# Row norm in the attention, one block for the finish, and two early loads, in a hybrid decoder layer on one core

## What is computed

```python
h = rmsnorm(x, g_mix_pre); proj = h @ w_in            # q, k, v and the RWKV inputs
o_att = attend(q, k4, v, lam)                         # differential attention, 4 heads of 128
o_att = rmsnorm(o_att, g_subln) * (1 - lam_init)      # per head and token
# RWKV: y from the delta-rule scan, 8 heads of 64
y = (y - mean) * rsqrt(var + GN_EPS)                  # per head and token
y = y * ln_x_w + ln_x_b
y = (y + bonus) * g
mix = concat([o_att, y]) @ w_o
x = x + rmsnorm(mix, g_mix_post)
x = x + rmsnorm(conv_ffn(rmsnorm(x, g_ffn_pre)), g_ffn_post)
x = x + rmsnorm((pe @ w_ple) * sigmoid(x @ w_ple_gate), g_ple)
```

## Time and profile before

| | us |
|---|---|
| median of 3 runs | 2096.89 (2096.22 to 2100.23) |
| profiled execution, device time | 2095.08 |
| its span | 2093.3 |
| mean granted clock of TensorE | 0.938 |
| TensorE busy | 1875.1 (90%) |
| VectorE busy | 1056.6 (50%) |
| ScalarE busy | 788.2 (38%) |
| GpSimd busy | 281.3 (13%) |

### The profile page before, as it was taken

One profiled execution on the slowest core, in us unless ns is written; L12 is line 12 of the kernel. 1 busy time (PEld: TensorE's weight loads), 2 busy tenths in 40 slices (PEclk: granted clock), 3 DMA queues, 4 the chain that ended last, 5 costly groups with the idle time before them and its releaser, 6 DMA issues.

```text
span 2093.3 us, 46480 instructions
## 1 busy us (share of the span) xinstructions
PE 1875.1 (90%) x19772; PEld 1781.1 (85%) x19772; DVE 1056.6 (50%) x1828; ACT 788.2 (38%) x1358; POOL 281.3 (13%) x288
## 2 busy tenths in 40 slices
PE   6999999599997488875499899999999999999996
PEld 5888888599996366664499899999999999999996
DVE  4355544235444466632326586654336766523655
ACT  4243323023320355531234555443335555422442
POOL 0011112069950000003000000000000000000000
PEclk9999999899999688886599999999999999999998
DMA  4234333620010877531124243323433422333343
GB/s 151 98 127 147 122 106 127 243 57 4 4 25 12 226 216 222 171 133 46 51 90 154 77 148 122 120 90 110 134 124 122 165 92 91 99 112 111 112 134 104
DMA packets 100620, 240.73 MB, mean 115 GB/s; under 512 B 14210, under 2 KB 18434, under 8 KB 100130
## 3 DMA queue, kind: packets, MB, share of 16 engines
q1 hardware_dynamic: 99554, 234.55, 35.0%
q10 hardware_dynamic: 864, 3.24, 0.4%
HBM read 189.54 MB, written 48.21 MB: 114 GB/s over the span
## 4 chain that ended last, share of the span: by engine, by line
PE 46%; DVE 2%; ACT 1%; issue 1%; DMA 0%; POOL 0%; SPq 0%; ACTq 0%; DVEq 0%
PE tl_acc L1970 44%; PE tl_ple L1970 1%; PE tl_wide L1945 0%; PE tl_wide L1936 0%; ACT tl_wh L2119 0%; DVE tl_tmp L2244 0%; DVE tl_gated L2307 0%; DVE tl_gated L2310 0%; DMA tl_raw<-dram_w_o 0%; ACT tl_sq_e L1982 0%; DVE tl_Y L2226 0%; DVE tl_Y L2217 0%; ACT tl_Hh L2088 0%; DVE tl_acc_e L2150 0%; DVE tl_wl L2290 0%
## 5 line engine op out<-in xcount | busy, mean ns | idle before, releaser
L1970 PE MATMUL tl_acc<-tl_Hh,tl_wh 128*128 128x264 f32 x1536 | 440.1, 287 | 7.3 <-DVE tl_Hl L2248 7.3
L1970 PE MATMUL tl_acc<-tl_Hh,tl_wl 128*128 128x264 f32 x1536 | 438.3, 285 | 0.0
L1970 PE MATMUL tl_acc<-tl_Hl,tl_wh 128*128 128x264 f32 x1536 | 438.2, 285 | 0.0
L2290 DVE TENSOR_TENSOR tl_wl<-tl_raw,tl_wh 128x1024 fp32r<-128x1024 f32 (+2 forms) x184 | 208.4, 1132 | 427.2 <-ACT tl_wh L2119 427.1
L2119 ACT ACTIVATE tl_wh<-tl_raw 128x1024 fp32r<-128x1024 f32 (+2 forms) x184 | 181.0, 984 | 503.0 <-PE tl_acc L1970 454.0
L1970 PEld LDWEIGHTS tl_acc<-tl_Hh,tl_wh 128*128 128x128 f32 x1536 | 290.3, 189 | 8.5 <-DVE tl_Hl L2248 8.3
L1970 PEld LDWEIGHTS tl_acc<-tl_Hh,tl_wl 128*128 128x128 f32 x1536 | 291.3, 190 | 0.0
L1970 PEld LDWEIGHTS tl_acc<-tl_Hl,tl_wh 128*128 128x128 f32 x1536 | 290.7, 189 | 0.0
L1970 PE MATMUL tl_acc<-tl_Gl,tl_wh 128*128 128x264 f32 x704 | 200.3, 285 | 0.0
L1970 PE MATMUL tl_acc<-tl_Gh,tl_wl 128*128 128x264 f32 x704 | 200.1, 284 | 0.0
L1970 PE MATMUL tl_acc<-tl_Gh,tl_wh 128*128 128x264 f32 x704 | 200.0, 284 | 0.0
(11 more groups left out here) (355 smaller groups left out, 4431.8 us busy)
## 6 DMA issues: line engine op xcount, KB each, us to landing
tl_raw<-dram_w_up SPq DMA_DIRECT2D x88, 512.0 KB, 3.6
...
```

Of the source, the lines that this page charges most:

```text
L1970: last = nc.tensor.matmul(out[:, n, 0:HP], w[:, u % 2, k, :], z, start=(begin and q == 0), stop=(end and q == 2))
L2290: tt(wl[:, u % 2, 0:kt], raw[:, u % 3, 0:kt], wh[:, u % 2, 0:kt].bitcast(F32), ALU.subtract).then_inc(S["residued"], 1)
```

## The change

- In the attention the first head's q and k are loaded and split inside the scan: SyncE issues the four loads, ScalarE makes the four high parts, GpSimd the four low parts. `dup`, `qs`, `kh` and `kl` are allocated outside of both stages.
- A block's weights are no longer scaled by 1/sum0: `wgt = p0 + p1 * (coefficient * sum0)`, one operation in place of two. `values` swaps its operands, so that a block's output has tokens on the partitions, and `leave` applies 1/sum0, once with a square that also sums along the row, and once as a copy.
- The attention's norm is taken from these sums: `root_rows`, `norm_rows`, `turn_rows` (eight transposes) and `keep_rows` (a copy with the gain), in the next head's steps 2, 3, 4 and 5. For the last head they stand at the end, together with the samples'. A head is stored whole.
- `rwkv_finish`, the small block, `rms_rows` and both `scale_split` become one block, `finish_rows`. The variance is made by a full-width matmul; root and reciprocal (`scale`, on VectorE) run over all 1056 columns; the bias is added to the bonus by GpSimd; the splits of O and Y into `Mh` and `Ml` stand in it.
- In the same block the first three units of `w_o` are loaded and two of them split; `tail` begins with unit 2.

```diff
-def attend(kit, a, proj, oT, ident, identb, causal, lam):
+def attend(kit, a, proj, oT, ident, identb, causal, lam, eps, g_subln, dup, qs, kh, kl):
...
-        dup = kit.sb(ctx, "ap_dup", [P, 2, 2, SEQ])
-        qs = kit.sb(ctx, "ap_qs", [P, 2, 2, SEQ], F32R)
-        kh = kit.sb(ctx, "ap_kh", [P, 2, 2, SEQ], F32R)
-        kl = kit.sb(ctx, "ap_kl", [P, 2, 2, SEQ], F32R)
...
             def load_qk(h):
-                if h:
-                    sp.wait_ge(S["low"], h * 4)
+                if h >= 2:
+                    sp.wait_ge(S["low"], (h - 1) * 4)
...
+            def store(h):
+                sp.wait_ge(S["o_kept"], h + 1)
+                sp.dma_start(oT[h][:, 0:SEQ], out[:]).then_inc(S["o_stored"], 16)
...
-            load_qk(0)
...
+                if s % NQ == 6 and 0 < h:
+                    store(h - 1)
+            store(HEADS - 1)
...
+                elif i == 3 and h:
+                    pe.wait_ge(S["o_kept"], h)
...
-                    last = nc.tensor.matmul(pv[:, 0:P], vt[:, h % 2, n, :], wT[:, s % 2, n, :],
+                    last = nc.tensor.matmul(pv[:, 0:P], wT[:, s % 2, n, :], vt[:, h % 2, n, :],
...
+            def turn_rows(h):
+                pe.wait_ge(S["normed"], h + 1)
+                pe.wait_ge(S["kept"], min(NQ * (h + 1) + 3, U))
+                for n in range(NQ):
+                    last = nc.tensor.transpose(tp[:, n, :], orow[:, h % 2, n, :], ident)
+                last.then_inc(S["o_turned"], 1)
...
+                if s % NQ == 4 and s >= NQ:
+                    turn_rows(s // NQ - 1)
...
-                nc.vector.tensor_scalar(small[:, b, 8:9], small[:, b, 7:8], neg_lam, None,
-                                        ALU.mult).then_inc(S["coefd"], 1)
+                nc.vector.tensor_scalar(small[:, s % 4, 8:9], small[:, s % 4, 7:8], neg_lam, small[:, s % 4, 4:5],
+                                        ALU.mult, ALU.mult).then_inc(S["coefd"], 1)
...
-                nc.vector.tensor_scalar(wgt[:, b, 0:keys], pexp[:, b, 0, 0:keys], small[:, b, 6:7], None,
-                                        ALU.mult).then_inc(S["w_first"], 1)
...
-                nc.vector.scalar_tensor_tensor(wgt[:, b, 0:keys], pexp[:, b, 1, 0:keys], small[:, b, 8:9],
-                                               wgt[:, b, 0:keys], ALU.mult, ALU.add).then_inc(S["weighted"], 1)
+                nc.vector.scalar_tensor_tensor(wgt[:, b, 0:keys], pexp[:, b, 1, 0:keys], small[:, s % 4, 8:9],
+                                               pexp[:, b, 0, 0:keys], ALU.mult, ALU.add).then_inc(S["weighted"], 1)
...
+            def norm_rows(h):
+                dve.wait_ge(S["rooted"], h + 1)
+                groups = slice(h % 2, h % 2 + (1 if h < HEADS - 1 else 2))
+                nc.vector.reciprocal(rms[:, groups], rms[:, groups]).then_inc(S["o_inverted"], 1)
+                dve.wait_ge(S["o_inverted"], h + 1)
+                nc.vector.tensor_tensor(orow[:, h % 2], orow[:, h % 2], rms[:, h % 2].unsqueeze(2).broadcast_to([P, NQ, P]),
+                                        ALU.mult).then_inc(S["normed"], 1)
...
+                if s % NQ == 3 and s >= NQ:
+                    norm_rows(s // NQ - 1)
...
+            norm_rows(HEADS - 1)
+            nc.vector.tensor_tensor(rows_out[:], rows_out[:], rms[:, 2].unsqueeze(2).broadcast_to([P, NB, P]),
+                                    ALU.mult).then_inc(Z["normed"], 1)
...
             def leave(s):
-                g, at = s // 4, (s % 4) * P
+                h, i = s // NQ, s % NQ
                 act.wait_ge(S["summed"], s + 1)
-                if s % 4 == 0 and g >= 2:
-                    act.wait_ge(half_out[g % 2], (g // 2) * 16)
-                nc.scalar.activation(out[:, g % 2, at:at + P], pv[:, 0:P], ACT.Copy).then_inc(S["evacuated"], 1)
+                if i == 0 and h >= 2:
+                    act.wait_ge(S["o_turned"], h - 1)
+                act.wait_ge(S["inverted"], s + 1)
+                if s:
+                    act.wait_ge(S["squared"], s)
+                nc.scalar.activation(sq[:], pv[:, 0:P], ACT.Square, scale=small[:, s % 4, 6:7],
+                                     accum_out=rms[:, h % 2, i:i + 1]).then_inc(S["squared"], 1)
+                nc.scalar.activation(orow[:, h % 2, i], pv[:, 0:P], ACT.Copy, scale=small[:, s % 4, 6:7])\
+                    .then_inc(S["evacuated"], 1)
+
+            def root_rows(h):
+                act.wait_ge(S["squared"], NQ * (h + 1))
+                groups = slice(h % 2, h % 2 + (1 if h < HEADS - 1 else 2))
+                if h == HEADS - 1:
+                    act.wait_ge(Z["squared"], NB)
+                nc.scalar.activation(rms[:, groups], rms[:, groups], ACT.Sqrt, bias=eps, scale=1.0 / P)\
+                    .then_inc(S["rooted"], 1)
+
+            def keep_rows(h):
+                act.wait_ge(S["o_turned"], h + 1)
+                if h:
+                    act.wait_ge(S["o_stored"], 16 * h)
+                else:
+                    act.wait_ge(S["gained"], 1)
+                nc.scalar.activation(out[:].rearrange("p (n t) -> p n t", t=P), tp[:], ACT.Copy, scale=gs[:])\
...
+                nc.scalar.activation(sq_s[:], one[:, 0:P], ACT.Square, accum_out=rms[:, 2, n:n + 1]).then_inc(Z["squared"], 1)
...
+                if s % NQ == 5 and s >= NQ:
+                    keep_rows(s // NQ - 1)
...
+                if s % NQ == 2 and s >= NQ:
+                    root_rows(s // NQ - 1)
...
+            for n in range(2):
+                src = proj[n * HEADS][:, 0:SEQ].rearrange("(c r) t -> r c t", c=2)
+                for rows in (slice(0, DH), slice(DH, P)):
+                    sp.dma_start(dup[rows, n], src).then_inc(S["qk_in"], 16)
...
+        @block.scalar
+        def _(act):
+            act.wait_ge(S["qk_in"], 64)
+            for n, dst in enumerate((qs, kh)):
+                for c in range(2):
+                    nc.scalar.activation(dst[:, 0, c], dup[:, n, c], ACT.Copy).then_inc(S["high"], 1)
+
+        @block.gpsimd
+        def _(pool):
+            for c in range(2):
+                pool.wait_ge(S["high"], c + 1)
+                nc.gpsimd.tensor_tensor(qs[DH:P, 0, c], dup[DH:P, 0, c], qs[DH:P, 0, c].bitcast(F32), ALU.subtract)\
+                    .then_inc(S["low"], 1)
+            pool.wait_ge(S["low"], 2)
+            for c in range(2):
+                pool.wait_ge(S["high"], c + 3)
+                nc.gpsimd.tensor_tensor(kl[:, 0, c], dup[:, 1, c], kh[:, 0, c].bitcast(F32), ALU.subtract)\
+                    .then_inc(S["low"], 1)
+            pool.wait_ge(S["low"], 4)
...
-def rwkv_finish(kit, a, spill, epsg, param, Y, ident, blockcol):
+def finish_rows(kit, a, spill, oT, epsg, param, Y, Mh, Ml, raw, wh, wl):
...
+            for p in range(NPAIR):
+                sp.dma_start(O[:, p], oT[p]).then_inc(o_in[p], 16)
+                sp.dma_start(BON[:, p], spill[0][:, p]).then_inc(bon_in[p], 16)
+                sp.dma_start(G[:, p], spill[1][:, p]).then_inc(g_in[p], 16)
+            for u in range(3):
+                sp.dma_start(raw[:, u].rearrange("p k m -> p (k m)"), a["w_o"][u]).then_inc(w_in[u], 16)
+            sp.wait_ge(w_in[2], 16)
...
+                for n in range(3):
+                    last = nc.tensor.matmul(pq[:, n, 0:T3], blk64[:], sq[:, p % 2, n * T3:(n + 1) * T3], start=True, stop=True)
...
+            def scale(p):
+                dve.wait_ge(S["rooted"], p + 1)
+                nc.vector.reciprocal(sd[:, p % 2], sd[:, p % 2]).then_inc(S["inverted"], 1)
+                dve.wait_ge(S["inverted"], p + 1)
+                tt(dev[:, p], dev[:, p], sd[:, p % 2], ALU.mult).then_inc(S["divided"], 1)
+                dve.wait_ge(S["divided"], p + 1)
+                dve.wait_ge(S["shifted"], p + 1)
+                nc.vector.scalar_tensor_tensor(dev[:, p], dev[:, p], param("ln_w", 4)[:, p:p + 1], BON[:, p],
+                                               ALU.mult, ALU.add).then_inc(S["affine"], 1)
+
+            def low(p):
+                dve.wait_ge(S["high"], p + 1)
+                tt(Ml[:, HEADS + p], Y[:, p], Mh[:, HEADS + p].bitcast(F32), ALU.subtract).then_inc(S["low"], 1)
+
+            def o_low(h):
+                dve.wait_ge(S["o_high"], h + 1)
+                tt(Ml[:, h], O[:, h], Mh[:, h].bitcast(F32), ALU.subtract).then_inc(S["o_low"], 1)
+            centre(1)
+            o_low(0)
+            scale(0)
+            centre(2)
+            o_low(1)
+            scale(1)
+            centre(3)
+            o_low(2)
+            scale(2)
+            o_low(3)
+            scale(3)
+            for u in range(2):
+                dve.wait_ge(S["rounded"], u + 1)
+                tt(wl[:, u], raw[:, u], wh[:, u].bitcast(F32), ALU.subtract).then_inc(S["residued"], 1)
             for p in range(NPAIR):
+                low(p)
...
+            for p in range(NPAIR):
+                pool.wait_ge(g_in[p], 16)
+                nc.gpsimd.tensor_tensor(Y[:, p], dev[:, p], G[:, p], ALU.mult).then_inc(S["gated"], 1)
...
```

(26 more changed lines are left out.)

201 lines of the change are left out of this document (104 added, 97 removed).

## The result

The changed kernel takes 2062.53 us (median, 2060.81 to 2066.21); beside it on the same chip the old one took 2098.56 (2096.22 to 2105.40). The ratio is 0.983, with a 95% interval of 0.980 to 0.985: 36 us or 1.7% faster. Forecast were 2068 and a range of 2049 to 2084. The profiled execution took 2063.8 us, its span is 2062.0, 31.3 less than before. The table and all that follows account for these 31.3 us of one pair of profiles, not for the 36 of the medians.

A forecast was written before the change was run, and what follows sets the result against it. Block-to-block latency was taken to bound the row norms, and nearly TensorE alone the attention. The terms -41.6 + 9.5 + 11 - 7.8 = -28.9 took 2095.08 to 2066.2 us, a median of 2068, range 2049 to 2084.

The forecast's parts named there:

- The finish: From the finish's first transfer to the tail's first matmul: 72.9 us in place of 114.5, -41.6 us, with VectorE's list longest.
- The port term: In the finish, GpSimd's gate multiplies and VectorE's operations with two SBUF inputs delay each other: 5 us (0 to 10).
- The end: End of attention: square, table load, root, reciprocal, multiplies, transposes, copy and store follow one another: +9.5 us (7 to 12).
- The start: Start of attention: shorter load queue brings the second head 11.8 us earlier, less 4.0 in the scan: -7.8 us.
- The scan's price: In the scan, GpSimd's four `low` slow VectorE's operations with two SBUF inputs: +4 us (0 to 9.4).
- Inside the attention: Table loads, transposes and the sample's squares, less the dropped VectorE operation: 3.5 us a head, +11 us (-2 to +20).
- The table loads: At step 2 of the next head, two loads for ScalarE's root make an exponential 2.0 us late, TensorE waiting.
- the lost operation: VectorE loses L1016 per attention step: 0.7 us gained at each head's start, 0.2 before the coefficients.
- The signs: Expected marks include head period 58.5 us, second head's copy at 713 to 714; wrong if attention's mean clock is below 0.8.
- (a): Rival in the finish: the wide reciprocal streams an element a cycle, 23.4 us less, 2045; chance 0.08.
- (b): Rival at the start: the first head's early split buys nothing, +6.7 us there, total 2082.5; chance 0.11.
- (c): Rival in the attention: TensorE's clock falls, no gain at 0.72, 2118 us at 0.65; chance 0.05.

The follow-up runs named there:

- e8: Against the changed kernel, the finish makes 1/sqrt by Ln and Exp on ScalarE in place of root and VectorE reciprocal; 2050.90 us.
- e2: Against the changed kernel, the first head's four q and k residues are made by VectorE at the attention's start, not GpSimd in the scan; 2063.04 us.
- e5: Against the changed kernel, VectorE gets back one operation per attention step, a multiply by 1.0 at the second weighting's old place; 2070.11 us.
- e6: Against the changed kernel, a copy replaces the row norm's root in heads 0 to 2, which removes six table loads; 2068.75 us.
- e10: Against the changed kernel, turn_rows of heads 0 to 2 makes one of its eight transposes; 2067.99 us.
- e9: Against the changed kernel, second head's q and k loaded in the scan, state stored from ScalarE's queue, finish with paired Ln and Exp; 2040.51 us.

## Why the prediction was right, point by point

*The finish* (-41.6 said, -41.7 measured) was right as a mechanism and near by size: its list on VectorE bounds it, and e8 shows that the four reciprocals, worked out from narrow rows, are what the list hangs on. That the last digit agrees is luck. The first `scale` begins at 16.4 us and not 12.9: `rf_blk` landed 3.8 us after its issue (1.9 before), and TensorE's second mean took 3.8 us for 2.0. The reciprocals gave back 1.4 and the instructions follow one another without the 0.04 us of gap that was charged. In the nine profiles with this finish it took 68.9 to 73.0 us, 71.0 in the mean. The port term (5 us) is seen in place: L1744 twice 2.7 and L1760's pair 4.64, each operation 1.25 without GpSimd, 5.0 us together. How much of the 42 us is the merging of blocks, and how much is the norm of the attention that moved out (and costs 7.7 and 10.1 us elsewhere), no run separates. The Trainium skill's repeat count of 8 (VectorE: DVE Perf Modes, First, the fixed hardware budget) gave an estimate of 8.8 us; the row says 6.74, and the measurement decides.

*The end* (+9.5, +10.1): the chain was as listed. The transposes took 1.97 and 1.92 us, 1.46 said. That row was misread: it is headed as 1.2 GHz, but the granted clock over its 1.46 us was 0.71; here it was 0.50 (1.2 GHz) from 932.8 to 936.5 us.

*The start* (-7.8, -6.1). SyncE's lead came as said (pages 8.7 us earlier, second head asked for 8.6 earlier). The mis-sized term is its landing: 13.8 us after the issue, 10.5 said. Most of the difference is the transfer itself and not what stands ahead of it: the sum put 2.1 MB at the 236 GB/s of a full queue and 1.5 us, 10.5 in all, but the same four transfers take 12.8 us with nothing ahead of them (648.10 to 660.88 above, and 677.30 to 690.12 before). The scan's price of +4 was +2.9 here, and e2 gives the cause: GpSimd's residues. Four instances of L1546 took 0.81 to 1.06 us for 0.42. Over the eight profiles of an unchanged scan the whole price was 2.9 to 6.5, 4.7 in the mean, so the +4 was the better number than this one profile says.

*Inside the attention* (+11, +7.7) the size is within the range said. In this pair of profiles the main terms stand where the sum put them, when each step's first exponential is compared with the one before. The table loads cost 2.12 us at each of steps 11, 19 and 27 (2.0 said). At steps 13, 21 and 29, where `turn_rows` stands, it is 0.0, 2.7 and 2.6 (1.5 each said). At steps 7, 8, 15, 16, 23 and 24 the lost operation gives 3.2 back (2.7 said), and e5 brings 3.3 of it back. What was wrong is to treat them as prices that can be taken off one by one: taking the table loads out gave nothing (e6), taking the transposes out gave nothing (e10), and putting the operation back cost 7.2, not 3 (e5). What the step missed is that TensorE's time there is no sum of its instructions: the same 1623 matmuls took 175.6 us or 179.6, as the granted clock changed between its two levels. At the same place of the same list, 11.8 us after step 10's exponential, the 18 matmuls of the coefficients took 2.12 us in the changed kernel and 3.81 in e9.

*The signs*: the first head's period from step 8 to step 16 is 56.4 us (55.3 before), the second's 58.3 (55.0); 58.5 was said. The clock over the attention is 0.82, above the 0.8 given as the sign of being wrong. The second head's copy came at 716.2, 713 to 714 said.

*The table load*: no drain shows in the kernel after either; the root starts 0.02 us behind the end of its load, and the load 0.01 us behind the activation before it. The Trainium skill (ScalarE: Activation LUTs, What ACT_TABLE_LOAD costs) names a drain beside the load; by the rows (928.48 + 1.28 = 929.76, root at 929.78) there is none.

*The rivals.* (a) fell with 6.74 us. (b) fell: undoing the early split costs 6.9 us. (c) fell: the clock over the attention is 0.82 where 0.72 was the point of no gain.

Open: the tail's -2.2 us. In all thirteen profiles of the changed tail it takes 1046.4 to 1047.8 us, with w_o's loads at the old place too (1046.9), against 1049.4 in the one profile of before. What makes the difference wasn't tried. The +0.9 before the scan lies within what this part varies by (645.5 to 653.2).
